# Recurrent stage of a two-block transformer kernel: decay rows moved to ScalarE, units 5 and 6 begun earlier, fillers at the gated rows

## What is computed

```python
x = _layer_norm(x, ln_emb_g, ln_emb_b)
proj = x @ w_in[l]
q_a, k_a, v_a, f_a, q_r, f_r, i_r, g_r = jnp.split(proj, SPLIT_POINTS, axis=-1)
logf_a = log_sigmoid(f_a + fox_f_bias[l])
o_a = _fox_attention(q_a, k_a, v_a, logf_a)
o_a = _rms_norm_heads(o_a, fox_norm_g[l])
logf_r = logaddexp(log(lb), log1p(-lb) + log_sigmoid(f_r))
o_r = _hgrn2_chunked(silu(q_r), -expm1(logf_r), i_r, logf_r)
o_r = _rms_norm_heads(o_r, hgrn_norm_g[l]) * silu(g_r)
mix = concatenate([o_a, o_r]) @ w_o[l]
x = _layer_norm(ALPHA * x + mix, ln_mix_g[l], ln_mix_b[l])
```

## Time and profile before

| | |
|---|---|
| median of 3 runs | 1367.94 us |
| lowest, highest | 1364.5, 1368.06 us |
| span of the profiled execution | 1365.2 us |
| TensorE busy | 1315.1 us (96%) |
| VectorE, ScalarE, GpSimd busy | 955.1, 728.6, 151.2 us |
| granted TensorE clock, mean | 0.985 of full speed |
| recurrent stage | about 1000 to 1160 us of the span |

### The profile page before, as it was taken

How to read it: one execution, slowest core, us unless ns; L and a number is a source line. 1 busy time by engine, 2 the same in 40 slices (tenths; PEclk the granted TensorE clock), 3 DMA queues, 4 the chain that set the end, 5 groups by cost and what they waited for, 6 DMA issues and landing times.

```text
span 1365.2 us, 19630 instructions
## 1 busy us (share of the span) xinstructions
PE 1315.1 (96%) x7433; PEld 1140.8 (84%) x7433; DVE 955.1 (70%) x1272; ACT 728.6 (53%) x995; POOL 151.2 (11%) x137
## 2 busy tenths in 40 slices
PE   8999999599999999999999999999998999999996
PEld 7888887488888888888898888888888988888884
DVE  6666676868766676666666677666679678787777
ACT  6444456766444455444567665444554543556662
POOL 2100002258300000000023210000004110000000
PEclk9999999899999999999999999999998999999998
DMA  8655644156655546556453356655524243455650
GB/s 276 224 185 188 199 148 141 34 146 189 215 194 184 186 154 215 186 192 196 165 176 123 103 193 209 197 186 186 183 93 124 94 154 124 147 192 193 206 184 31
DMA packets 165425, 229.24 MB, mean 168 GB/s; under 512 B 4027, under 2 KB 135354, under 8 KB 165248
## 3 DMA queue, kind: packets, MB, share of 16 engines
q1 hardware_dynamic: 163120, 221.33, 49.8%
q0 software_dynamic: 2160, 7.24, 1.8%
q10 hardware_dynamic: 96, 0.02, 0.0%
HBM read 227.52 MB, written 1.05 MB: 167 GB/s over the span
## 4 chain that ended last, share of the span: by engine, by line
PE 84%; DVE 9%; ACT 3%; issue 2%; POOL 1%; DMA 0%; SPq 0%; DVEq 0%; ACTq 0%
PE ps L428 27%; PE ps L435 14%; PE ps L374 13%; PE ps L375 12%; PE ps L376 12%; DVE w_lo L304 3%; PE ps L1377 1%; PE ps L673 1%; PE ps L2202 1%; ACT w_hi L296 1%; POOL p_sb L1464 1%; DMA x_tok<-in_x_dram 0%; PE ps L1340 0%; PE ps L773 0%; POOL arena L2064 0%
## 5 line engine op out<-in xcount | busy, mean ns | idle before, releaser
L304 DVE TENSOR_TENSOR w_lo<-raw,w_hi 128x2048 fp32r<-128x2048 f32 x208 | 482.6, 2322 | 100.3 <-ACT w_hi L296 100.2
L428 PE MATMUL ps<-h_both,w_hi 128*128 128x512 f32 x1744 | 419.2, 392 | 1.1 <-DVE h_both L709 0.7
L296 ACT ACTIVATE w_hi<-raw 128x2048 fp32r<-128x2048 f32 x208 | 396.2, 1906 | 22.3 <-PE ps L376 20.7
L428 PEld LDWEIGHTS ps<-h_both,w_hi 128*128 128x128 f32 x1744 | 323.8, 189 | 66.4 <-DVE h_both L709 1.3
L435 PEld LDWEIGHTS ps<-h_both,w_lo 128*128 128x128 f32 x1744 | 224.7, 191 | 8.9
L435 PE MATMUL ps<-h_both,w_lo 128*128 128x256 f32 x1744 | 228.1, 283 | 0.0
L896 ACT ACTIVATE s_sb<-ps 128x512 f32<-128x512 f32 x88 | 52.5, 597 | 231.1 <-PE ps L435 231.1
L374 PE MATMUL ps<-w_hi,gu_hi 128*128 128x512 f32 x400 | 156.5, 391 | 0.8 <-DVE w_lo L304 0.8
L375 PE MATMUL ps<-w_hi,gu_lo 128*128 128x512 f32 x400 | 156.3, 391 | 0.0
L376 PE MATMUL ps<-w_lo,gu_hi 128*128 128x512 f32 x400 | 155.7, 389 | 0.0
L902 DVE TENSOR_TENSOR s_sb<-ps,s_sb 128x512 f32<-128x512 f32 x88 | 60.8, 690 | 102.6 <-ACT s_sb L896 102.6
(11 more groups left out here) (343 smaller groups left out, 1689.6 us busy)
## 6 DMA issues: line engine op xcount, KB each, us to landing
raw<-in_ffn_w_up_dram SPq DMA_DIRECT2D x44, 1024.0 KB, 5.4
raw<-in_ffn_w_down_dram SPq DMA_DIRECT2D x44, 1024.0 KB, 4.8
raw<-in_ffn_w_gate_dram SPq DMA_DIRECT2D x43, 1024.0 KB, 5.4
raw<-in_w_up_dram SPq DMA_DIRECT2D x22, 1024.0 KB, 5.1
raw<-in_w_in_dram SPq DMA_DIRECT2D x14, 1024.0 KB, 5.3
raw<-in_odd_w_qkv_dram SPq DMA_DIRECT2D x12, 1024.0 KB, 5.1
raw<-in_w_down_dram SPq DMA_DIRECT2D x11, 1024.0 KB, 5.0
raw<-in_even_w_in_dram SPq DMA_DIRECT2D x4, 1024.0 KB, 5.3
```

The source lines that it names most:

```text
L296: act.activation(w_hi[slot][:, :], raw[slot][:, :], ACT.Copy).then_inc(w_hi_ready, 1)
L304: dve.tensor_tensor(w_lo[slot][:, :], raw[slot][:, :], w_hi[slot][:, :].bitcast(F32), ALU.subtract).then_inc(w_lo_ready, 1)
L428: pe.matmul(PS[:, bank, :], a[:, k, t * P:(t + 1) * P], h_both[:, :, k, :], start=k == 0, stop=False, skip_group_check=True)
```

## The change

ScalarE forms the decay rows in place of VectorE: five Identity activations with per-partition scale and bias, read from a table of constants that is six columns wider. The order in `REC` is changed: split 5 goes ahead of the gate sum, units 5 and 6 are begun ahead of the diagonal and the level products, split 7 goes behind the decay rows, unit 7 is begun ahead of the products of level 1, and the second half of unit 10 goes ahead of turn 2. At `gated-0` seven matmuls of the first `rec_out` unit, whose results nobody reads, are put around the two groups of transposes, with the waits that they need.

```diff
-            t[row:row + 8, C_FOX + 4:C_FOX + 8] = (-8, 0, 0, 1)
-            t[row + 32:row + 40, C_FOX + 4:C_FOX + 8] = (0, 1, 8, 0)
+            t[row:row + 8, C_FOX + 12:C_FOX + 14] = (0, 1)
+            t[row + 32:row + 40, C_FOX + 12:C_FOX + 14] = (8, 0)
+            t[row:row + 8, C_FOX + 4:C_FOX + 8] = -8 * t[row:row + 8, C_FOX:C_FOX + 4]
+            t[row + 32:row + 40, C_FOX + 8:C_FOX + 12] = t[row + 32:row + 40, C_FOX:C_FOX + 4]
...
-                dlink(dve, dve.tensor_tensor_scan(f_c, ones, f_m, 0.0, ALU.mult, ALU.add))
-
-            def dve_decay(self, dve):
-
-                dve.tensor_scalar(fox_query, f_c, fox_col[2], fox_col[3], ALU.mult, ALU.add)
-                dlink(dve, dve.tensor_scalar(f_m, f_c, fox_col[0], fox_col[1], ALU.mult, ALU.add))
-                dve.tensor_tensor(fox_key, f_m.unsqueeze(1).to_broadcast([P, 4, S]),
-                                  fox_pick.unsqueeze(2).to_broadcast([P, 4, S]), ALU.mult).then_inc(self.bias_ready, 1)
+                dve.tensor_tensor_scan(f_c, ones, f_m, 0.0, ALU.mult, ALU.add).then_inc(self.sum_ready, 1)
+
+            def act_decay(self, act):
+
+                act.wait_ge(self.sum_ready, 1)
+                act.activation(fox_query, f_c, ACT.Identity, bias=fox_query_bias, scale=fox_query_scale)
+                for j in range(4):
+                    m = act.activation(fox_key[:, j, :], f_c, ACT.Identity, bias=fox_key_bias[j], scale=fox_key_scale[j])
+                m.then_inc(self.bias_ready, 1)
...
-                    "gates-0 split_hi-4 split_lo-4 unit-2 k-0 split_hi-5 chunk_exps-0 fox_chain-0 unit-3 silu_q-0 "
-                    "chunks-0 split_lo-5 unit-4 diag-0 mm64-0 read64-0 diag_read-0 split_hi-6 split_lo-6 first-5 "
-                    "mm128-0 read128-0 level-0 split_hi-7 split_lo-7 fox_decay-0 second-5 level_mm-0 level-1 "
-                    "level_read-0 first-6 scores-0 max-0 exp-0 second-6 level_mm-1 level-2 level_read-1 split_hi-8 "
-                    "split_lo-8 first-7 second-7 turn-0 hi-0 lo-0 level_mm-2 level-3 level_read-2 split_hi-9 "
+                    "gates-0 split_hi-4 split_lo-4 unit-2 k-0 split_hi-5 unit-3 chunk_exps-0 split_lo-5 fox_chain-0 silu_q-0 "
+                    "chunks-0 split_hi-6 split_lo-6 unit-4 first-5 diag-0 mm64-0 read64-0 diag_read-0 second-5 "
+                    "fox_decay-0 split_hi-7 mm128-0 read128-0 level-0 split_lo-7 first-6 level_mm-0 second-6 level-1 "
+                    "level_read-0 scores-0 first-7 max-0 exp-0 level_mm-1 level-2 level_read-1 split_hi-8 "
+                    "split_lo-8 second-7 turn-0 hi-0 lo-0 level_mm-2 level-3 level_read-2 split_hi-9 "
...
-                    "split_hi-11 split_lo-11 scores-2 max-2 exp-2 first-10 level_mm-5 level_read-5 turn-2 hi-2 lo-2 "
-                    "second-10 scores-3 max-3 exp-3 split_hi-12 split_lo-12 unit-11 values-2 turn-3 split_hi-13 "
+                    "split_hi-11 split_lo-11 scores-2 max-2 exp-2 first-10 level_mm-5 level_read-5 second-10 turn-2 hi-2 "
+                    "lo-2 scores-3 max-3 exp-3 split_hi-12 split_lo-12 unit-11 values-2 turn-3 split_hi-13 "
...
                         pe.wait_ge(rec.read_done, 2 + len(LEVELS))
-                    n_gated.pe(pe, half=n)
+                        pe.wait_ge(att_fox.exp_done, 8)
+                        weight_fill(pe, rec_proj.u0, 4, bank=0)
+                        n_gated.pe_turn(pe, 0)
+                        weight_fill(pe, rec_proj.u0, 3, bank=0)
+                        n_gated.pe_turn(pe, 1)
+                    else:
+                        n_gated.pe(pe, half=n)
```

More of the change, by code:

```diff
@@ L64 @@
 C_FOX = C_CAUSAL + P + S
-C_LEVEL = C_FOX + 8
+C_LEVEL = C_FOX + 14
 C_N = C_LEVEL + 64 * len(LEVELS)
@@ L179, in build @@
         causal_mask = consts[:, C_CAUSAL:C_CAUSAL + P + S]
-        fox_pick = consts[:, C_FOX:C_FOX + 4]
-        fox_col = [consts[:, C_FOX + 4 + n:C_FOX + 5 + n] for n in range(4)]
+        fox_key_scale, fox_key_bias = ([consts[:, C_FOX + 4 * n + j:C_FOX + 4 * n + j + 1] for j in range(4)] for n in (1, 2))
+        fox_query_scale, fox_query_bias = (consts[:, C_FOX + n:C_FOX + n + 1] for n in (12, 13))
         mix_gain = consts[:, C_ROPE:C_ROPE + DM]
@@ L534, in norm_fill, with weight_fill @@
                 pe.matmul(PS[:, 3, :], h_hi[:, n % KC, 0:P], h_hi[:, 0:2, :], start=True, stop=True)
-        def weight_fill(pe, n, count):
+        def weight_fill(pe, n, count, bank=3):
             slot = n % RING
@@ L540, in weight_fill @@
             for _ in range(count):
-                pe.matmul(PS[:, 3, :], w_hi[slot][:, 0:P], w_hi[slot][:, 0:512], start=True, stop=True)
+                pe.matmul(PS[:, bank, :], w_hi[slot][:, 0:P], w_hi[slot][:, 0:512], start=True, stop=True)
         def tok_unit(pe, n, half, banks, ready=None, done=None, between=None, parts=(0, 1), src=None, off=0,
@@ L1950, in __init__ @@
                 self.f_chain = sem("fox_f_chain")
+                self.sum_ready = sem("fox_sum_ready")
                 self.bias_ready = sem("fox_bias_ready")
@@ L2695, in _ @@
                     rec.act_k(act)
+                elif what == "fox_decay":
+                    fox.act_decay(act)
                 elif what == "chunk_exps":
@@ L2778, in _ @@
                     fox.dve_chain(dve)
-                elif what == "fox_decay":
-                    fox.dve_decay(dve)
                 elif what == "gates":
```

## The result

The changed kernel took 1372.20 us (median of 5 runs, 1370.38 to 1372.76). The kernel before took 1366.58 on the same chip (median of 5, 1364.5 to 1368.06). The ratio is 1.005, with a 95% interval of 1.0033 to 1.0068: slower by 0.5%, where I had forecast +1.0 us and called the most likely outcome one that a measurement can't tell from no change.

The account below looks back on a forecast made before the run. TensorE was taken as the bound, busy 1315.1 of 1365.2 us, leaving only idleness and half clock to win. Terms +4.0 - 1.3 - 1.7 = +1.0 us on 1367.94 gave 1368.9 us, range 1364.5 to 1372.5.

Parts of the forecast that it names:

- term D: Turn 2 behind second 10: wait of 1.0 goes, 1.4 comes ahead of scores 3, clock stays full; -1.3 us.
- term B: Order ahead of level 0: ScalarE's later exponentials make TensorE idle 7.0 us instead of 2.08, same clock loss; +4.0 us.
- Rival 2: Ahead of level 0: GpSimd doesn't get between VectorE's pair; -0.85 us, 1367.1 us; chance 0.16.
- rival 1: Behind turn 2: the clock falls all the same; +2.7, 1370.6 us; chance 0.22.
- Term G: Gated rows: seven filler matmuls keep the clock full behind the transposes, idle time only filled; -1.7 us.
- Rival 4: Gated rows: fillers stand on the path at half clock; sum +4.3, 1372.2 us; chance 0.12.
- slower: Whole kernel: measurably slower, beyond about 0.3% or 4.1 us; chance 0.12.
- VectorE's decay rows: Recurrent stage: taking three decay instructions off VectorE saves nothing by itself, as no TensorE wait names the bias rows.

Follow-up runs that it names:

- e4_early_exp: Changed kernel with ScalarE's level-0 exponentials moved early, behind split 6 and ahead of unit 4's copy; ratio 0.995 to the kernel before.
- e11_fill_cover: Changed kernel with thirty unread products ahead of level 0, reading unit 6, which is split long before; ratio 1.0008 to the kernel before.
- e3_turn: Kernel before with only the second half of unit 10 put ahead of turn 2; ratio 0.9986 to the kernel before.
- e6_decay_back: Changed kernel with the decay rows formed by VectorE again, at the new place in the order; ratio 1.001 to the kernel before.
- e7_split7_later: Changed kernel with the high split of unit 7 behind level 0's exponentials on ScalarE; ratio 1.0009 to the kernel before.
- e10_fill_long: Changed kernel with thirty unread products ahead of level 0, reading unit 7, whose low split comes behind level 0's products; ratio 1.0104 to the kernel before.
- e9_fill_level: Kernel before with the decay rows on ScalarE behind split 7 and nine unread products ahead of level 0; ratio 0.998 to the kernel before.
- e1_table: Kernel before with only the constants table six columns wider; ratio 0.9998 to the kernel before.
- e2_fill: Kernel before with only the seven fillers at the gated rows; ratio 0.999 to the kernel before.
- e8_both: Changed kernel with early level-0 exponentials, unit 8's splits further ahead, turn 2's old order and low split 11 behind its exponentials; ratio 0.9942 to the kernel before.
- e0_changed: Changed kernel measured and profiled once more, on another chip, nothing altered; ratio 1.0028 to the kernel before.

## Why the prediction was wrong

The step that failed is term D: -1.3, on a clock that would stay full behind the wait of 1.4; the clock fell, and the term came out at +0.3. Beside it stand the bank of unit 8, which the sum had at nothing (+0.8), and term B, 0.4 too small. Together they turn +1.0 into +3.8 in these two profiles. The mechanism ahead of level 0, the largest term, was right. The +5.6 between the two profiled executions holds 1.8 us more from ahead of the stage, and all terms were set against a single execution of before, which is taken up under "The base".

Times of after below have the 1.76 us taken off by which it came late into the stage (1006.60 less 1004.84).

**Ahead of level 0: right.** First 5 covers the wait ahead of the diagonal. TensorE reached level 0 at 1047.70 (1056.55 less 7.09 less 1.76; forecast 1047.7). The chain on ScalarE came as worked out (its timeline in after):

```profile
1045.84 0.60 ACT L1224 ACTIVATE qk_hi<-ps 128x512 fp32r<-128x512 f32 x1 [7.32 <-PE ps L378]
1046.33 0.59 ACT L2009 ACTIVATE xn_tok<-p_sb,consts 128x256 f32<-128x256 f32 x1
1046.83 2.08 ACT L2011 ACTIVATE t_feat<-p_sb,consts 128x256 f32<-128x256 f32 x4
1048.80 1.91 ACT L298 ACTIVATE w_hi<-raw 128x2048 fp32r<-128x2048 f32 x1
1050.72 1.28 ACT L2183 ACT_TABLE_LOAD   x1
1052.01 0.63 ACT L2183 ACTIVATE arena<-arena 128x512 f32<-128x512 f32 x1
1052.55 0.61 ACT L2184 ACTIVATE arena<-arena 128x512 f32<-128x512 f32 x1
```

The five activations take 2.47 us (1046.33 to 1048.80; forecast 2.3), with no table load ahead of them. The exponentials end at 1051.4 (1053.16 less 1.76; forecast 1051.5). GpSimd met VectorE's pair, as in the earlier trace rows:

```profile
1053.24 2.51 POOL L2068 TENSOR_TENSOR arena<-arena 128x1024 f32<-128x1024 f32 x1 [6.84 <-ACT arena L2184]
```
```profile
1053.20 0.69 DVE L2193 TENSOR_TENSOR arena<-arena 128x512 f32<-128x512 f32 x1 [5.37 <-ACT arena L2184]
1053.80 2.49 DVE L2194 TENSOR_TENSOR arena<-qk_feat,arena 128x512 f32<-128x512 f32 x1
```

Level 0 began at 1054.79 (forecast 1054.7), behind 7.09 us (forecast 7.0). Rival 2, that GpSimd doesn't come between, fell. That the meeting cost what I forecast is luck in part: the subtraction took 2.51 us and not 1.89, and VectorE's pair ended 0.54 behind it (1056.29 against 1055.75) and not 1.15, and the two errors cancel. The cited rule of the Trainium skill (ScalarE: Activation LUTs, What ACT_TABLE_LOAD costs) of a drain of 1.38 us besides the load isn't borne out by these rows: split 7 ends at 1050.71, the load starts at 1050.72 and lasts 1.28, and the exponential starts 0.01 behind it. Its 93 ns for each pointer operand agrees roughly: an activation with two takes 0.59 us, one without 0.42.

**Term B: right in kind, 0.4 too small.** The level-2 products started at 1068.24 before and at 1074.36 in after, with the same work behind both: 6.12 less 1.76, +4.36, against +4.0. TensorE's timeline of before has the two places that this term and the next are read from:

```profile
1068.24 1.90 PE L2202 MATMUL ps<-arena 128*128 128x64 f32 x16
...
1070.24 0.36 PE L374 MATMUL ps<-h_both,w_hi 128*128 128x256 f32 x1
```

**The bank of unit 8: missed, +0.8.** The first half of unit 8 follows the level-2 products and waits until VectorE has copied unit 7 out of the bank that it reuses (the trace of after names no releaser; that of e4_early_exp has a wait of 1.17 at this place and names this copy). VectorE's timeline in before, then in after:

```profile
1068.91 1.23 DVE L1251 TENSOR_TENSOR rowvec_r<-ps,v_hi 128x1024 fp32r<-128x1024 f32 x1 [1.78 <-ACT v_hi L1222]
```
```profile
1073.66 2.27 DVE L306 TENSOR_TENSOR w_lo<-raw,w_hi 128x2048 fp32r<-128x2048 f32 x1
1075.85 1.22 DVE L1253 TENSOR_TENSOR rowvec_r<-ps,v_hi 128x1024 fp32r<-128x1024 f32 x1
```

The copy ends at 1077.07 and unit 8 begins at 1077.17, 0.91 behind the level-2 products. Before, the copy ended at 1070.14 and unit 8 began at 1070.24 too, but that was only 0.10 behind the level-2 products (1068.24 and 1.90). With first 7 moved ahead of level 1, TensorE comes from level 1 to level 2 in 5.20 us (1069.16 to 1074.36) in place of 7.90 (1060.34 to 1068.24), while VectorE still needs 5.9 from level 2's first product to the end of that copy (1071.19 to 1077.07). I followed the chain of ScalarE and of the level products, but not that of the banks: for a unit that is begun earlier in the queue, who frees the bank of the next one was never asked. By here after was 5.17 behind (1077.17 less 1070.24 less 1.76).

**Term D: rival 1 came, +0.3 where I took -1.3.** The idle time came as forecast (1.40), but the clock fell behind it and cost 1.7. Turn 3 started at 1113.18 before and at 1120.42 in after (TensorE's timelines):

```profile
1113.18 0.88 PE L1377 MATMUL ps<-consts,p_sb 128*128 128x128 f32 x6
```
```profile
1120.42 0.87 PE L1379 MATMUL ps<-consts,p_sb 128*128 128x128 f32 x6
```

7.24 less 1.76 is 5.48, 0.31 more than at unit 8. This is the largest error, 1.6 us. A single profile can't give this term. Of the eight profiles with the 1.40 us wait the clock fell in three (the changed kernel twice, e11_fill_cover) and stayed full in five (e3_turn, e4_early_exp, e6_decay_back, e7_split7_later, e10_fill_long). Of the five with the old wait of 1.0, it fell in two (before, e9_fill_level). On average the term is about +0.3 (1.40 and 3/8 of 1.7, less 1.05 and 2/5 of 1.7).

**Term G: right in this pair, -1.65 against -1.7, and by luck.** The transposes of `gated-1` started at 1142.54 before and at 1148.13 in after, 5.59 less 1.76, 3.83 behind:

```profile
1142.54 1.03 PE L784 MATMUL ps<-consts,xn_tok 128*128 128x128 f32 x8
```
```profile
1148.13 1.03 PE L786 MATMUL ps<-consts,xn_tok 128*128 128x128 f32 x8
```

But the loss that the fillers save stood in one of five profiles without them, so their mean is nearer 0.3 than 1.7.

**The sum.** 5.17 + 0.31 - 1.65 = +3.8, the stage's difference, where I had +1.0. Rival 4 (fillers on the path at half clock) gives the measured time and did not happen at the gated rows; only in e10_fill_long, elsewhere, does such a filler show.

**The base: one execution stood for all.** I set every term against the profiled execution of before, which had lost the clock three times, 6.8 us in the stage. Four profiles have its order at level 0 (before, e1_table, e2_fill, e3_turn); the clock fell there in two, and the other two waited 1.7 for scores 0 in its place. The changed kernel has no such luck: behind 7 us the clock fell in both profiles. So on average the kernel before loses 0.5 x 3.4 + 0.5 x 1.7 = 2.6 us there and not 3.4, and about 1.0 at turn 2 and the gated rows (2/5 and 1/5 of 1.7) and not 3.4. Term B goes up by 0.85, and G from -1.7 to -0.3. An estimate of the average effect from these rows is 4.36 + 0.85 + 0.8 + 0.3 - 0.3 = +6.0 us, from few profiles. Measured were +5.3 (means of 5 and 5 runs, 1371.91 and 1366.58) and +3.9 (of 12 and 29). The estimate is somewhat high, and how often the clock falls isn't settled by so few profiles. And with a sum of +1.0 beside losses that come in steps of 1.7 and 3.4, a chance of 0.12 for "slower" was too little.

**VectorE's decay rows** were put down at nothing, because no wait named them. e1_table shows that this holds only where half clock covers VectorE's queue: at full clock scores 0 wait 1.7 us for the copy behind them.

**What wasn't tried**: which condition makes the clock fall behind a wait of 0.8 to 2.1 us in one execution and not in another. That stays open. Nor was the bank of unit 8 tried by itself: e8_both moves two things, so the 0.8 rests on the timelines alone.

## What to carry to other kernels

When steps are moved ahead for one engine, write out the new queue of every engine that feeds it: here TensorE's order improved, while ScalarE's put the exponentials of the next product behind a copy, five activations and a split, and what was taken out of that queue again came off the wait nearly one to one. Moving the exponentials alone ahead turned +3.9 us into -5.9, each against the kernel before. And a wait that is missing from one profile may be covered by a clock loss of that execution: before costing an edit at nothing, or at a clock loss's full value, see how it stands in a second profile.

## What the runs showed of the hardware

The clock losses in the stage came in steps of about 1.7 us (0, 1.7, 3.4, 5.1 and 6.8 in fourteen profiles) and differ from execution to execution: the same kernel order lost 6.8 us (before) or nothing (e1_table), behind the same waits of 0.8 to 2.1 us. What falls inside a long wait isn't paid: of the 5.1 us lost around level 0 in e0_changed, the stage with fillers in that wait (e11_fill_cover) gave back 3.4.

Behind the waits of 4.6 to 7.1 us at level 0 the clock was at half in four profiles of four (the changed kernel twice, e6_decay_back, e7_split7_later). With thirty products that nobody reads in the wait of 7.1, level 0 ran at full clock (2.00 us in place of 3.64), in the one profile taken. With nine in the wait of 2.1 it did too, but so it did in three of five profiles without them. Thirty with a wait of their own cost 10 us more than the changed kernel.

A VectorE product that takes 0.68 us alone took 2.49 when GpSimd's subtraction had started 0.04 us behind the instruction ahead of it; GpSimd's took 2.51 then, against 1.89 in the earlier trace rows. The product ended 0.54 behind the subtraction.
